# Four weight halves of an output product split behind sums 1 to 4 instead of behind sum 4, and the gates' halves one row sooner, in a fused three-layer block kernel

## What is computed

```python
# first block
mix = jnp.concatenate([y_ssd, y_fnet, y_pool], axis=-1) @ w_out
x = post_norm(x, mix, g1, ln1_g, ln1_b)
...
# hybrid layer, twice (l = 0, 1)
proj = rms_norm(h, g_mix) @ w_in
...
h = h + jnp.concatenate([att, hm], axis=-1) @ w_out
u = rms_norm(h, g_mlp) @ w_ff1
h = h + jnp.square(jax.nn.relu(u)) @ w_ff2
gate = jax.nn.sigmoid(rms_norm(h, g_ple) @ w_ple_gate + b_ple_gate)
return h + gate * (p_i @ w_ple)
```

## Time and profile before

| | |
|---|---|
| median of three runs | 2129.61 us (2128.34 to 2133.23) |
| the profiled execution, its own time | 2128.61 us |
| its span (first to last instruction) | 2126.8 us, mean granted clock 0.986 |
| busy: PE / DVE / ACT / POOL | 97% / 54% / 41% / 37% |
| output product, first block: second part of sum 0 to end of sum 7 | 263.5 to 300.6 us |
| output product, layers 0 and 1: from sum 0's second part to the FFN | 949.8 to 989.8, 1668.9 to 1709.0 us |
| gates, layer 0 and layer 1 | 1359.5 to 1415.6, 2077.9 to 2121.5 us |

### The profile page before, as it was taken

How to read it: one execution, slowest core, us unless ns; L and a number is a source line. 1 busy time by engine, 2 the same in 40 slices (tenths; PEclk the granted TensorE clock), 3 DMA queues, 4 the chain that set the end, 5 groups by cost and what they waited for, 6 DMA issues and landing times.

```text
span 2126.8 us, 25850 instructions
## 1 busy us (share of the span) xinstructions
PE 2057.0 (97%) x10348; PEld 1613.3 (76%) x10348; DVE 1139.4 (54%) x1991; ACT 862.2 (41%) x1369; POOL 788.4 (37%) x404
## 2 busy tenths in 40 slices
PE   6999999999999989999999999998999999999998
PEld 3877667888887757787888888676687788888867
DVE  5366769995664698834523121447886453222134
ACT  4543334342333656753322222346667332222232
POOL 0343114675563224420544444002344034444420
PEclk9999999999999989999999999999999999999999
DMA  8124621232322201212333322121111233332212
GB/s 317 60 100 159 217 81 60 91 108 99 99 89 76 80 21 40 80 41 80 109 100 99 100 99 99 64 91 51 41 41 40 80 92 116 92 97 89 99 60 99
DMA packets 186663, 194.24 MB, mean 91 GB/s; under 512 B 8496, under 2 KB 181936, under 8 KB 186160
## 3 DMA queue, kind: packets, MB, share of 16 engines
q1 hardware_dynamic: 185968, 189.44, 27.2%
q10 hardware_dynamic: 576, 3.15, 0.4%
HBM read 190.48 MB, written 2.10 MB: 91 GB/s over the span
## 4 chain that ended last, share of the span: by engine, by line
PE 83%; DVE 6%; ACT 2%; issue 1%; POOL 1%; ACTq 0%; DVEq 0%
PE ps L803 19%; PE ps L804 19%; PE ps L805 19%; PE ps L820 3%; PE ps L822 2%; PE ps L821 2%; PE ps L848 1%; PE ps L1255 1%; PE ps L1310 1%; DVE arena_m L2719 1%; PE ps L1399 1%; PE ps L1419 1%; PE ps L1343 1%; PE ps L837 1%; PE ps L1413 1%; PE ps L838 1%
## 5 line engine op out<-in xcount | busy, mean ns | idle before, releaser
L2808 POOL TENSOR_TENSOR wl<-ring,wh 128x1024 fp32r<-128x1024 f32 (+1 forms) x252 | 622.0, 2474 | 981.6 <-ACT wh L1454 980.9
L1454 ACT ACTIVATE wh<-ring 128x1024 fp32r<-128x1024 f32 (+2 forms) x294 | 304.1, 1044 | 332.5 <-PE ps L805 256.7
L803 PE MATMUL ps<-xh,wh 128*128 128x512 f32 (+1 forms) x976 | 383.1, 393 | 1.9 <-POOL wl L2808 1.7
L805 PE MATMUL ps<-xh,wl 128*128 128x512 f32 (+1 forms) x976 | 380.7, 390 | 0.0
L804 PE MATMUL ps<-xl,wh 128*128 128x512 f32 (+1 forms) x976 | 380.5, 390 | 0.0
L803 PE MATMUL ps<-acts,wh 128*128 128x512 f32 x880 | 346.0, 393 | 9.5 <-DVE wl L1970 8.7
L804 PE MATMUL ps<-acts,wh 128*128 128x512 f32 x880 | 343.6, 390 | 0.0
L805 PE MATMUL ps<-acts,wl 128*128 128x512 f32 x880 | 343.5, 390 | 0.0
L2437 DVE SCALAR_TENSOR_TENSOR mix<-ps,par,mix 128x441 f32<-128x441 f32 (+2 forms) x352 | 213.6, 691 | 30.2 <-ACT mix L1685 30.1
L803 PEld LDWEIGHTS ps<-xh,wh 128*128 128x128 f32 (+1 forms) x976 | 183.0, 187 | 46.4 <-issue 7.8
L805 PEld LDWEIGHTS ps<-xh,wl 128*128 128x128 f32 (+1 forms) x976 | 183.0, 187 | 39.2
(11 more groups left out here) (434 smaller groups left out, 3094.0 us busy)
## 6 DMA issues: line engine op xcount, KB each, us to landing
ring<-in_w_ff_dram SPq DMA_DIRECT2D x64, 1024.0 KB, 5.2
ring<-in_w_in_dram SPq DMA_DIRECT2D x28, 1024.0 KB, 5.3
ring<-in_ffn_w_up_dram SPq DMA_DIRECT2D x22, 1024.0 KB, 4.8
ring<-in_w_ada_dram SPq DMA_DIRECT2D x17, 1024.0 KB, 5.1
ring<-in_w_out_dram SPq DMA_DIRECT2D x12, 1024.0 KB, 4.9
ring<-in_ffn_w_down_dram SPq DMA_DIRECT2D x8, 1024.0 KB, 4.7
ring<-in_w_ple_gate_dram SPq DMA_DIRECT2D x8, 1024.0 KB, 4.7
early<-in_w_ada_dram SPq DMA_DIRECT2D x7, 1024.0 KB, 10.7
```

Source lines behind the costliest of these rows:

```text
L803: t.matmul(b[0:m, 0:n], s.hi[:, k, a:a + m], x2[0][:, k, :], start=k == ks[0], stop=False)
L805: i = t.matmul(b[0:m, 0:n], s.lo[:, k, a:a + m], x2[0][:, k, :], start=False, stop=k == ks[-1])
L1454: a.activation(s.hi[:, :, c], s.ap[:, :, c], ACT.Copy).then_inc(*up("hi", "hi", name, hf))
L2808: p.tensor_tensor(s.lo[:, :, c], s.ap[:, :, c], s.hi[:, :, c].bitcast(F32), ALU.subtract).then_inc(*up("lo_pool", "lo", name, hf))
```

## The change

Every second part of a split sum now registers a use too, of the same key and half, with `ahead` 3, and the first parts give theirs `ahead` 0. Between gate 6 and the first rows of the next layer a use of the last half of the gate weights is registered, without a product, so that the planner orders this half ahead of those of ("tok", 1, 0). In ACT's list of the output product, `high` of rows 1 to 3 stands behind the `feed` of the row before; rows 4 to 7 stay in front of their own. In the gates' lists of ACT and DVE, `high` and `low` of key 0 stand in front of row 0's work and those of key j + 1 at the end of row j.

```diff
--- before.py
+++ after.py
@@ -809,8 +809,10 @@
             def part(key, name, hf, x2, second, where=None, xk=None, keep=False, ks=range(8)):
 
                 s = W.named[name]
-                if not second:
-                    use(key, name, (hf,), True, 3 if keep else 0)
+                if second:
+                    use(key, name, (hf,))
+                else:
+                    use(key, name, (hf,), True, 0)
                     take(key, keep, where)
                     e.wait_ge(*at("lo", name, hf))
                 b, a = ps(key), 128 * hf
@@ -1264,6 +1266,7 @@
                         for i in range(4):
                             square("g1", i, b, n.sq2)
                     if l == 0 and j == 6:
+                        use(("pg", l, j), ("pg", l, 3), (1,), False)
                         first_rows(1, range(3))
                 if l == 0:
                     for i, rows in ((4, (3,)), (5, (4, 5)), (6, (6,)), (7, (7,))):
@@ -1730,8 +1733,11 @@
                     e.wait_ge(*done(("pg", 0, 7)))
                 layer_scalar(e, a, l, high_half, out_of)
                 for j in range(8):
-                    high(("wo", l, j))
+                    if j >= 4:
+                        high(("wo", l, j))
                     feed(("m", l), j, taken(("wo", l, j)), ("g_mlp_2", l), n.sq2, xh, done(("mo", l, 3)))
+                    if j < 3:
+                        high(("wo", l, j + 1))
 
                 def up2(g):
                     for jl in range(8):
@@ -1770,11 +1776,13 @@
                 root(("p", l), n.rs2)
                 for j in range(2, 8, 2):
                     out_of(("pw", l, j), n.pw[:, j, :])
+                high(("pg", l, 0))
                 for j in range(8):
                     e.wait_ge(*taken(("pg", l, j)))
                     a.activation(n.gates[:, j % 2, :], n.gates[:, j % 2, :], ACT.Sigmoid,
                                  bias=pc("b_ple_gate_2", 8 * l + j)).then_inc(*up("act", "gate", l, j))
-                    high(("pg", l, j))
+                    if j < 7:
+                        high(("pg", l, j + 1))
                     if (l, j) == (0, 7):
                         a.activation(roots[:, 0:1], eps[:, 0:1], ACT.Sqrt).then_inc(*up("act"))
                     if l == 0:
@@ -2518,6 +2526,7 @@
                 for j in range(1, 8, 2):
                     e.wait_ge(*done(("pw", l, j)))
                     v.tensor_copy(n.pw[:, j, :], ps(("pw", l, j))[:, :]).then_inc(*free(("pw", l, j)))
+                low(("pg", l, 0))
                 e.wait_ge(*at("rs", ("p", l)))
                 for j in range(8):
                     g = n.gates[:, j % 2, :]
@@ -2528,7 +2537,8 @@
                     v.tensor_tensor(g, g, n.pw[:, j, :], ALU.mult).then_inc(*up("vec"))
                     after()
                     v.tensor_tensor(h[:, j, :], h[:, j, :], g, ALU.add).then_inc(*up("vec", "h3", l, j))
-                    low(("pg", l, j))
+                    if j < 7:
+                        low(("pg", l, j + 1))
                     if l == 0:
                         feed("g1", j, ("g_mix_2", 1), xh, xl)
```

## The result

The changed kernel takes **2112.43 us** (median of four runs, 2109.01 to 2113.46) where the kernel before took 2131.42 in runs on the same chip (2128.34 to 2134.22). The ratio is 0.9907, with a 95% interval of 0.9894 to 0.992: 19 us, or 0.93%, faster. The forecast was 18.8 us and 2110.8 us, with a range of 2107 to 2116. The interval of the ratio stands for 17 to 23 us, so that the two agree within 0.2 us is in part luck; the gains place by place, further down, are the closer test.

What follows compares the result with a forecast made beforehand. TensorE, busy 97% of the span, was taken as the bound, so only its idle time and lower-clock products could yield. 5.85 + 5.9 + 0.2 + 6.85 = 18.8 us off the 2129.61 median gives 2110.8 us, range 2107 to 2116.

Steps and rivals of the forecast that it cites:

- The output product, layers 0 and 1: Second block: lo's split one a row remove the stall at sum 4; sum 5 starts 5.85 and 5.9 us sooner.
- The wait at the fourth square: Output product, behind sum 4: the fourth square waits 0.2 to 0.3 us for row 3's square on ACT.
- rival 1: Output-product squares: a new wait replaces part of the old, 0.3 us per 0.1 on DVE's row; 2117.6 us, 10%.
- The first block: Output product of the first block: its remaining wait on DVE's split goes, 0.2 us, with 0 and 0.5 as ends.
- Gates and first rows: Layer 0 gates: halves one row ahead end the next layer's first-rows wait; gate 7 starts 6.85 us sooner.
- Rival 2: First rows still wait because hand-overs before gate 0 delay the last lo; 3 to 4 us given back, 2114.5 us, 10%.
- The clock's part: Lower-clock losses behind the waits: 1.6 us at sum 4 in each layer, 2.3 in the first rows, 5.5 together.
- PE's busy time: Sign over the whole kernel: PE's busy time down by about 5 us, its idle time by about 14.
- from row 5 on DVE is paced by PE: Output product, layer 0: row 5 adds at 973.1 as sum 5 ends, and DVE follows PE from there.
- rival 4: Output product, both layers: row order itself bounds, slower from a 6.7 us row; 2134.4 us at 7.5, 3%.
- rival 5: The change doesn't do what it says, planner's lists stay as before; 2129.6 us, 2%.
- Rival 3: Three more lower-clock stretches elsewhere, 1.6 us each, 2115.6 us, or one or two fewer, 2108; 5%.

Runs made afterwards that it cites:

- the longer row: Changed kernel with each lo of output-product rows 1 to 3 subtracted a second time on DVE, both layers; 2124.89 us, ratio 0.9966 to the kernel before.
- the output product alone: Kernel before with only the planner's uses of the split sums' second parts, gates and ACT's text unchanged; 2119.23 us, ratio 0.9939.
- the mixer's dummies: Changed kernel with three dummy products at the mixer's 3.2 us wait, in either layer; 2118.29 us, ratio 0.9942 to the kernel before.
- the eighteen dummies in the kernel before: Kernel before with 18 dummy products on PE at each of the three lo waits; 2158.97 us, ratio 1.0127.
- the gates alone: Kernel before with only the gates' part: halves one row sooner and the extra use of the last gate half; 2124.82 us, ratio 0.9967.
- the four dummies: Kernel before with 4 dummy products on PE at each of the three lo waits, lo's no sooner; 2125.03 us, ratio 0.9973.
- the last gate half's order: Changed kernel without the added use of gate tile 3's second half between gate 6 and the first rows; 2110.62 us, ratio 0.9907.

## Why the prediction was right, by its steps

**The output product, layers 0 and 1 (5.85 and 5.9 us): 6.1 and 6.1.** The chain is the one that was worked out: sum 4 starts with no wait, sum 5 stands 6.68 us behind it (6.7 forecast), and a row of DVE is 4.09 us (4.1). The wait at the fourth square is there too, 0.15 us where I took 0.2 to 0.3. It is too short for the list of waits, which the prediction named as its sign, but the timeline shows it when only the first four records of the squares are asked for, first after, then before:

```profile
969.58 0.79 PE L907 MATMUL ps<-arena_f,con 128*32 128x512 f32 x4
```

```profile
972.30 0.64 PE L905 MATMUL ps<-arena_f,con 128*32 128x512 f32 x4
```

With all four squares ready they start together and take 0.64 us; in the changed kernel the fourth starts 0.16 later, at about 969.75, just behind the end of row 3's square on ACT at 969.07 + 0.63 = 969.70:

```profile
969.07 0.63 ACT L1477 ACTIVATE arena_f<-h 128x512 f32<-128x512 f32 x1 [1.89 <-DVE h L2488]
```

So the squares need 970.73 - 969.58 = 1.15 us instead of 1.0, in layer 1 as well (1677.34 - 1676.19), and the row has nothing in reserve: what it grows by, three times over, goes straight to PE, as the longer row showed (3.78 us for 3 x 1.26). This is the prediction's own rule in rival 1, 0.3 us for every 0.1 on the row, and it holds from the start.

**The first block (0.2 us): not told apart.** No wait for a lo made by DVE is left in the list, so it went; 0.2 us can't be told from drifts of that size elsewhere.

**Gates and first rows (6.85): 6.9.** DVE on these rows, against the earlier trace rows, the pair of lo's in front of gate 0 and single ones behind it:

```profile
1361.99 2.36 DVE L1978 TENSOR_TENSOR wl<-ring,wh 128x1024 fp32r<-128x1024 f32 x2 [5.16 <-ACT wh L1457]
1364.27 0.68 DVE L2534 TENSOR_TENSOR arena_p<-ps,arena_f 128x512 f32<-128x512 f32 x1
...
1369.15 0.69 DVE L2534 TENSOR_TENSOR arena_p<-ps,arena_f 128x512 f32<-128x512 f32 x1
...
1384.43 0.69 DVE L2534 TENSOR_TENSOR arena_p<-ps,arena_f 128x512 f32<-128x512 f32 x1 [0.47 <-PE ps L805]
...
1391.10 0.69 DVE L2534 TENSOR_TENSOR arena_p<-ps,arena_f 128x512 f32<-128x512 f32 x1 [1.70 <-PE ps L805]
...
1393.92 1.22 DVE L1978 TENSOR_TENSOR wl<-ring,wh 128x1024 fp32r<-128x1024 f32 x1
```

All is 2.6 us sooner than before here, by what came earlier. With that shift alone row 0 would have started at 1365.33 - 2.6 = 1362.7; it starts at 1364.27, so the two halves delay it by 1.5 us, as forecast. A row takes 4.88 us (5.06 forecast), the delay is made up by row 4, the first that waits for PE (forecast: row 4). The last lo ends at 1393.92 + 1.22 = 1395.14, and PE wants it at 1396.34: 1.2 us of slack, as forecast. The products took 4.31 us (4.3 to 4.5). Rival 2, that the first rows still wait, has therefore nothing for it.

**The clock's part (1.6 + 1.6 + 2.3 = 5.5).** Shown, both by the clock of 1.00 in the changed kernel's three places and by the dummies, which bring back 5.8 us without any sooner lo, in the same three places and sizes. Whether such an excess might turn up elsewhere instead is a question of its own; were all of it to come back, the gain would be 18.8 - 5.5 = 13.3 us. The medians do not bear that out: 19.0. In single executions there is something to it. The low-clock stretches at 306 and 931 come and go, and they move a profile by 1.6 and 3.1 us. The total time at the lower clock within the span fell from 59.4 us before to 50.6 and 52.9 in the two profiles of the changed kernel, by 8.8 and 6.5, where the three stretches that went held 13.6. So a third to a half of that time came back at other places; the stretch at 931 alone has 6.8. In the last section the reader finds which kernels had that stretch; whether the change makes it likelier is open.

**PE's busy time** was to fall by 5 and its idle time by 14. They fell by 3.0 and 12.1. Of the 2 us missing in the busy time, 3.1 less 1.6 are the products that ran slow at 931 and those that no longer did at 306. Of the 1.9 missing in the idle time, 1.3 are at the start, ahead of anything that the change touches, and 0.6 a longer wait of L1154 at 316 (1.4 instead of 0.8).

**Points missed.** First, I followed the lists through the planner and did not see that ACT's hunk of the output product orders nothing anew. Second, I wrote that from row 5 on DVE is paced by PE. The timeline has it otherwise:

```profile
981.93 0.69 DVE L2488 TENSOR_TENSOR h<-h,ps 128x512 f32<-128x512 f32 x1 [1.24 <-PE ps L805]
```

That is the first add behind row 0 that waits for PE, and it is a row later than I wrote, row 6. It cost nothing.

**The rivals.** Rival 1 exists as a mechanism but didn't occur, rivals 2, 4 and 5 left no sign in any run. Rival 3 occurred in the profiled execution (one stretch more, worth 3.1 us, one less, worth 1.6), and not in a size that the medians show.

## What to carry to other kernels

A long wait of TensorE for a piece of preparation had two prices here: the wait (4.33 to 4.35 us), and the products behind it that run at a lower granted clock (0.52 and 0.50 behind the two of layer 0, 0.51 in 1685.1 to 1688.5 behind the one of layer 1); 13.3 and 5.5 us over three waits, and both went when the preparation was dealt out one piece a row instead of four at the end. When pieces are moved ahead, lay out the row (add, square, copy, hi, xl, lo) with durations of the trace, compare it with the rate at which PE takes the rows, and look for who wants the results of the delayed rows: here it is the fourth square, and 1.26 us on the row costs 12.2 us, all that the output products had won. A short wait hides in a line that merges several products; ask the timeline for the first few alone. In a kernel whose TensorE is busy for 97%, judge by medians and put a ledger of start times beside the two profiles, because single executions differ by stretches at the lower clock that no edit touched (here worth 1.6 and 3.1 us).

## What the runs showed of the hardware that I had not expected

**The clock fell while PE was at work.** PE was busy for all of 6 us and then for all of 8 us, and in the second the granted clock is 0.57:

```profile
925.00:931.00 6.00, 6.00 (x49) 5.19 (x48) 2.93 (x6) 5.54 (x9) 2.68 (x3) 1.00 0.01 3
931.00:939.00 8.00, 8.00 (x30) 6.96 (x31) 0.99 (x4) 0.61 (x3) 0.00 (x0) 0.57 0.00 0
```

PE's timeline there, of the changed kernel and then, in a fence of its own, of the kernel before:

```profile
929.14 4.87 PE L1434 MATMUL ps<-con,arena_m 128*128 128x2 f32 x32
933.88 0.77 PE L822 MATMUL ps<-xh,wh 128*128 128x512 f32 x1
934.45 0.63 PE L823 MATMUL ps<-xl,wh 128*128 128x512 f32 x1
934.88 0.63 PE L824 MATMUL ps<-xh,wl 128*128 128x512 f32 x1
```

```profile
928.94 3.63 PE L1431 MATMUL ps<-con,arena_m 128*128 128x2 f32 x32
```

The same 32 products of two columns take 4.87 us in the one and 3.63 in the other, and the full-sized ones behind them take 0.63 us a piece instead of 0.39. No wait precedes it. What comes ahead of the fall is a series of products in which PE is busy but moves only two columns a product. The falls at sum 4 of layer 0 and at the first rows in the kernel before had a wait of over 4 us ahead of them (4.35 and 4.33 us, then 0.52 and 0.50); this one had none. Whether the small products have to do with it isn't shown: every kernel has the same series. Of the ten executions profiled, five show the stretch in this length (the changed kernel twice, the output product alone, the longer row, the mixer's dummies; granted clock 0.57 to 0.72 in 931 to 939), one has it half as long (the eighteen dummies in the kernel before; 0.79), and four have none (the kernel before, the gates alone, the four dummies, the last gate half's order; 1.00). The kernels with the change in the output product have it in five of six, the others in one of four, a shorter one. Since the work ahead of 931 differs only in the first block's halves, no run here tells whether that is more than chance.

**A dummy product can cost four times the real one.** A 128x512 product of plain fp32 operands took 0.87 us in a series of 18, and 3.60 / 4 = 0.90 in one of four, where the kernel's products of rounded halves follow each other at 0.23 us (963.82 to 964.05). Dummies that are to fill a wait must be counted at their own price.

**Filling a wait with dummies was worth something by itself**, 5.8 us of 2131 at three waits of over 4 us, where the bank they write was free before the wait. Behind a wait for a bank they only delayed: 4.54 us in either layer, and a kernel 6 us slower.
